# Group B's input projection as seven float32 block products instead of eight, and an earlier copy between the layers

## The reference

```python
for l in range(2):
    h = rms_norm(x, norm1_g[l])
    qa,ka,va, qb,kb,vb, qc,kc,vc = split(h @ w_in[l])        # 2304 columns, 768 for each group A, B, C
    oa = neighbourhood_attention(qa, ka, va)                 # 4 heads of 64
    ob = dilated_attention(qb, kb, vb)                       # 4 heads
    oc = gqa_attention(rope(qc), rope(kc), vc)               # 8 heads, 2 of keys and values
    x = x + [rms_norm(oa) | rms_norm(ob) | rms_norm(oc)] @ w_out[l]
    x = x + hier_moe(rms_norm(x, norm2_g[l]))                # 32 experts, two of one group for each token
```

## Time and profile before

| | us |
|---|---|
| median of 3 runs | 1152.03 (1151.15 to 1152.05) |
| the profiled execution | 1151.47 |
| its span, first to last instruction | 1149.6 |
| TensorE busy in it | 980.4 (85%) |
| VectorE busy | 291.0 (25%) |
| ScalarE busy | 178.7 (16%) |
| DMA, mean rate | 380 GB/s |
| chain that ended last, TensorE's share | 65% |
| the same, DMA's share | 30% |

### The profile page before, as it was taken

The page is one execution under the profiler, slowest core; times in us unless marked ns, Lnnn a source line. Parts: engine busy times, 40 slices in busy tenths (PEclk is TensorE's granted clock), DMA queues, the critical chain, the costliest instruction groups (busy, mean ns, idle before and its releaser), DMA issues.

```text
span 1149.6 us, 13653 instructions
## 1 busy us (share of the span) xinstructions
PE 980.4 (85%) x5402; PEld 460.5 (40%) x5402; DVE 291.0 (25%) x798; ACT 178.7 (16%) x444; POOL 54.0 (5%) x108
## 2 busy tenths in 40 slices
PE   8999999997887947549999999999969779474687
PEld 5556644353343413113356656444524234131242
DVE  4446552111110110001145555421111101100011
ACT  1344311110010100001024343111100001000110
POOL 2121100000000000000021111000000000000000
PEclk9999999999898977868999999999989889787899
DMA  9962999999999999999998248999999999999997
GB/s 319 351 253 110 364 335 421 427 427 428 428 426 427 428 428 427 428 427 421 397 397 312 100 179 351 366 419 427 428 427 428 428 428 427 428 427 428 428 419 290
DMA packets 64760, 437.08 MB, mean 380 GB/s; under 512 B 11230, under 2 KB 15670, under 8 KB 34230
## 3 DMA queue, kind: packets, MB, share of 16 engines
q1 hardware_dynamic: 64645, 436.16, 92.5%
q10 hardware_dynamic: 48, 0.01, 0.0%
HBM read 435.10 MB, written 1.44 MB: 380 GB/s over the span
## 4 chain that ended last, share of the span: by engine, by line
PE 65%; DMA 30%; DVE 2%; SPq 1%; POOL 1%; issue 1%; ACT 0%; POOLq 0%; DVEq 0%
PE bank L1105 33%; DMA ring<-in_w_down 15%; DMA ring<-in_w_gate 10%; PE bank L797 9%; DMA ring<-in_w_up 5%; PE bank L1131 5%; PE bank L929 5%; PE bank L1057 3%; PE bank L756 2%; PE bank L875 1%; PE bank L865 1%; SPq L518 1%; PE bank L897 1%; PE bank L957 1%; PE bank L1123 1%
## 5 line engine op out<-in xcount | busy, mean ns | idle before, releaser
L1105 PE MATMUL bank<-ring,work 128*32 128x512 f32 (+2 forms) x2608 | 481.5, 663 | 135.6 <-DMA ring<-in_w_up 51.2
L1105 PEld LDWEIGHTS bank<-ring,work 128*32 128x32 f32 (+2 forms) x2608 | 145.1, 130 | 400.7 <-issue 398.1
L797 PE MATMUL bank<-ring,hT 128*128 128x512 f32 (+1 forms) x384 | 128.3, 488 | 1.2 <-DVE hT L1474 1.2
L797 PEld LDWEIGHTS bank<-ring,hT 128*128 128x128 f32 x384 | 71.2, 190 | 48.3 <-issue 42.2
L1131 PE MATMUL bank<-work 128*128 128x512 f32 x176 | 81.4, 603 | 2.4 <-ACT work L1427 1.6
L1105 PE MATMUL bank<-work 128*32 128x512 f32 (+1 forms) x176 | 78.2, 594 | 4.1 <-DMA ring<-in_w_up 4.1
L1057 PEld LDWEIGHTS bank<-work,h 128*128 128x128 f32 x640 | 75.1, 192 | 14.5 <-issue 13.7
L1105 PE MATMUL bank<-kept,work 128*32 128x512 f32 (+2 forms) x160 | 68.2, 622 | 13.7 <-DMA ring<-in_w_down 13.7
L1057 PE MATMUL bank<-work,h 128*128 128x128 f32 x640 | 79.1, 277 | 0.0
L1898 DVE COPY work<-bank 128x512 f32<-128x512 f32 x20 | 13.8, 692 | 248.0 <-PE bank L1105 248.0
L1893 DVE TENSOR_TENSOR work<-work,bank 128x512 f32<-128x512 f32 x22 | 15.1, 687 | 213.8 <-PE bank L1105 213.8
(11 more groups left out here) (218 smaller groups left out, 736.0 us busy)
## 6 DMA issues: line engine op xcount, KB each, us to landing
ring<-in_w_gate SPq DMA_DIRECT2D x42, 2048.0 KB, 25.0
ring<-in_w_down SPq DMA_DIRECT2D x38, 2048.0 KB, 23.5
ring<-in_w_up SPq DMA_DIRECT2D x36, 2048.0 KB, 29.7
ring<-in_w_up SPq DMA_DIRECT2D x36, 1024.0 KB, 14.7
ring<-in_w_down SPq DMA_DIRECT2D x28, 1024.0 KB, 10.4
ring<-in_w_gate SPq DMA_DIRECT2D x20, 1024.0 KB, 8.7
ring<-in_w_in SPq DMA_DIRECT2D x8, 1536.0 KB, 12.9
ring<-in_w_out SPq DMA_DIRECT2D x8, 1024.0 KB, 17.1
```

The lines of the kernel that those rows point to most:

```text
L797: last = matmul(bank[6 + i % 2][:, 0:c1 - c0], hT[:, k, t * P:t * P + P], group_in(l, gi)[:, k, c0:c1], start=(k == 0), stop=(k == KD - 1))
L1105: last = nc.tensor.matmul(bank[b][e * w:e * w + w, :], lhs[:, k, e * w:e * w + w], rows(pos, k_count // 2)[:, kk, n * 512:n * 512 + 512], ...
```

## The change

Group B's product is cut in two row blocks, two halves of the features and two halves of the columns: `LEFT` (256 to 640) and `RIGHT` (640 to 768 and 0 to 256, in that order), 384 each. Eight products of blocks, each 4 chunks deep and 384 columns wide, are replaced by seven (`block_1` to `block_7`) of row blocks or their sums with weight blocks or their sums. VectorE forms the four row sums (`rows_summed`), and four weight sums (`term_1` to `term_4`; `term_3` overwrites the right columns of the upper weights). The products are added up in SBUF, scaled by `rstd`, in two buffers `partial(l, t)`: VectorE's steps named `..._added`, `..._kept` and `..._done`, and one on ScalarE (`first_block_kept`). `head_squares` for B reads the finished values in SBUF instead of PSUM. The first output products wait for `v_proj` alone.

Row sums take one piece of the ring and terms with the partial sums three, none of them loaded, until the last columns of B are done (`v_proj`, 12 a layer).

The order on VectorE also changes: `normalised(l, 4)` comes ahead of `greatest(l, 5)`, and the right columns of row block 1 are finished ahead of those of row block 0. Between the layers, `half_turned(1, 0, 1)` moves from ahead of projection 0 to its middle, beside `half_turned(1, 1, 1)`, and the copies of the first two turned parts (`rows_turned`) move from behind the four sums into x to a place between the second and the third.

```diff
@@ -122,7 +122,7 @@
         if key in QUARTERED:
             used[pos] += 3
         for i in range(pos, pos + n):
-            used[i] += i < pos + (2 if n == 3 else 1)
+            used[i] += loaded and i < pos + (2 if n == 3 else 1)
             freed[i], when[i] = done, time
         plan[key] = (pos, [used[i] for i in range(pos, pos + n)], sorted(waits.items()))
...
@@ -133,6 +133,8 @@
             take((l, "in", g), 3, ("p_proj", 12 * l + 4 * g + 4), t0 + 4 * g + 4, ring)
         for n, j in enumerate(OUT_PIECES):
             take((l, "out", j), 1, ("p_out", 12 * l + (4, 4, 8, 12)[n]), t0 + (16, 16, 26, 30)[n], ring)
+        for name, n in (("terms", 3), ("sums", 1)):
+            take((l, name), n, ("v_proj", 12 * l + 12), t0 + 13, ring, loaded=False)
         for n, (name, count, time) in enumerate(BESIDE_FREE):
             freed[PIECES + n], when[PIECES + n] = (name, (l + 1) * count), t0 + time
         for i, it in enumerate(TIME):
...
@@ -337,6 +342,30 @@
         def group_in(l, g):
             pos = PLAN[l, "in", g][0]
             return ring[:, pos * PIECE:(pos + 3) * PIECE].rearrange("p (k c) -> p k c", k=KD)
+        TERM = 4 * 384
+        LEFT, RIGHT = (256, 640), ((640, 768, 0), (0, 256, 128))
+        def row_block(t, half):
+            return hT[:, 4 * half:4 * half + 4, t * P:t * P + P]
+        def row_sum(l, n):
+            pos = PLAN[l, "sums"][0]
+            return ring[:, pos * PIECE + n * 512:pos * PIECE + n * 512 + 512].rearrange("p (k s) -> p k s", k=4)
+        def term(l, n):
+            at = PLAN[l, "terms"][0] * PIECE + n * TERM
+            return ring[:, at:at + TERM].rearrange("p (k c) -> p k c", k=4)
+        def partial(l, t):
+            at = PLAN[l, "terms"][0] * PIECE + 3 * TERM + t * 384
+            return ring[:, at:at + 384]
+        def weight_block(l, half):
+            return group_in(l, 2)[:, 4 * half:4 * half + 4]
         def rows(pos, k):
...
@@ -782,8 +811,7 @@
                     pe.wait_ge(a_sq, 12 * l + i - 1)
                 for k in range(KD):
                     if i == 0 and k == 4:
-                        if l == 0:
-                            half_turned(l, 1, 0)
+                        half_turned(l, *((1, 0) if l == 0 else (0, 1)))
                         half_turned(l, 1, 1)
                     if i < 2 and k % 4 == 0:
                         pe.wait_ge(v_xT, x_turned(l, t, k // 4))
@@ -797,6 +825,57 @@
                     last = matmul(bank[6 + i % 2][:, 0:c1 - c0], hT[:, k, t * P:t * P + P],
                                   group_in(l, gi)[:, k, c0:c1], start=(k == 0), stop=(k == KD - 1))
                 last.then_inc(p_proj, 1)
+            def block_product(b, left, right, done):
+                for lo, src in right:
+                    for k in range(4):
+                        last = matmul(bank[b][:, lo:lo + src.shape[-1]], left[:, k], src[:, k], start=(k == 0), stop=(k == 3))
+                last.then_inc(done, 1)
+            def left_columns(l, half):
+                return ((0, weight_block(l, half)[:, :, LEFT[0]:LEFT[1]]),)
+            def right_columns(l, half):
+                return [(lo, weight_block(l, half)[:, :, c0:c1]) for c0, c1, lo in RIGHT]
+            def block_1(l):
+                pos, count, _ = PLAN[l, "in", 2]
+                pe.wait_ge(landed[pos], 16 * count[0])
+                pe.wait_ge(v_proj, 12 * l + 7)
+                pe.wait_ge(a_sq, 12 * l + 7)
+                block_product(6, row_block(0, 0), left_columns(l, 0), p_block)
+            def block_6(l):
+                pe.wait_ge(v_terms, 4 * l + 2)
+                pe.wait_ge(v_proj, 12 * l + 8)
+                pe.wait_ge(a_sq, 12 * l + 8)
+                block_product(7, row_sum(l, 1), ((0, term(l, 1)),), p_block)
+            def block_2(l):
+                pos, count, _ = PLAN[l, "in", 2]
+                pe.wait_ge(landed[pos + 1], 16 * count[1])
+                pe.wait_ge(v_block, 4 * l + 1)
+                pe.wait_ge(a_block, l + 1)
+                block_product(6, row_block(0, 1), left_columns(l, 1), p_proj)
+            def block_7(l):
+                pe.wait_ge(v_terms, 4 * l + 3)
+                pe.wait_ge(v_block, 4 * l + 2)
+                block_product(7, row_sum(l, 2), right_columns(l, 0), p_block)
+            def block_4(l):
+                pe.wait_ge(v_terms, 4 * l + 4)
+                pe.wait_ge(v_proj, 12 * l + 9)
+                block_product(6, row_block(1, 1), ((0, term(l, 2)),), p_proj)
+            def block_5(l):
+                pe.wait_ge(v_block, 4 * l + 3)
+                block_product(7, row_sum(l, 0), ((0, term(l, 0)),), p_proj)
+            def block_3(l):
+                pe.wait_ge(v_proj, 12 * l + 10)
+                block_product(6, row_sum(l, 3), right_columns(l, 1), p_proj)
             def gains_turned(l, b):
                 if l == 0:
@@ -916,8 +995,7 @@
                 g, t, half = OUTS[n]
                 pos0, chunk0, count = CHUNKS[g]
                 if n < 2:
-                    pe.wait_ge(v_proj, 12 * l + 11 + n)
-                    pe.wait_ge(a_sq, 12 * l + 11 + n)
+                    pe.wait_ge(v_proj, 12 * l + 12)
...
@@ -965,7 +1043,7 @@
                     gains_turned(0, 7)
                 if l == 0:
                     half_turned(l, 0, 0)
-                half_turned(l, 0, 1)
+                    half_turned(l, 0, 1)
                 project(l, 0)
                 project(l, 1)
                 project(l, 2)
@@ -989,19 +1067,22 @@
                 values(l, 1)
                 scores(l, 3)
                 turn_keys(l, 1)
-                project(l, 8)
+                block_1(l)
+                block_6(l)
+                block_2(l)
                 turn_queries(l, 1)
                 softmax_turned(l, 2)
                 softmax_turned(l, 3)
-                project(l, 9)
+                block_7(l)
+                block_4(l)
                 values(l, 2)
                 squares(l, 0)
                 scores(l, 4)
                 values(l, 3)
                 scores(l, 5)
-                project(l, 10)
+                block_5(l)
                 turn_keys(l, 2)
-                project(l, 11)
+                block_3(l)
                 softmax_turned(l, 4)
                 squares(l, 1)
...
@@ -1256,6 +1337,8 @@
             def head_squares(l, i):
                 name, t, (c0, c1) = unit(i)
+                if i >= 10:
+                    t = 11 - i
                 which = ("k" if i % 4 < 2 else "q") + name
                 if which == "qC":
                     dst, n = lengths["qC0" if t == 0 else "qC1"], 512
@@ -1269,7 +1352,19 @@
                     act.wait_ge(p_turn, turned(l, "qA"))
                 if which == "qB":
                     act.wait_ge(v_len, len(LENGTHS) * l + LENGTHS.index("kB") + 1)
+                if name == "B":
+                    activation(dst, qk_b[:, t, c0:c0 + 256], ACT.Square).then_inc(a_sq, 1)
+                    return
                 activation(dst, bank[6 + i % 2][:, 0:n], ACT.Square, scale=rstd[:, t:t + 1]).then_inc(a_sq, 1)
+            def first_block_kept(l):
+                for name, value in PLAN[l, "terms"][2]:
+                    act.wait_ge(frees[name], value)
+                act.wait_ge(g_rstd, rooted(l, "x1"))
+                act.wait_ge(p_block, 3 * l + 1)
+                act.wait_ge(v_block, 4 * l + 1)
+                nc.scalar.mul(partial(l, 1), bank[6][:, 0:384], rstd[:, 1:2]).then_inc(a_block, 1)
             def keys_turned(l, gi):
                 name = "k" + GROUPS[gi]
@@ -1371,6 +1466,7 @@
                 heads_mixed(l, 1)
                 exponentials(l, 3)
                 keys_turned(l, 1)
+                first_block_kept(l)
                 head_squares(l, 8)
                 queries_turned(l, 1)
...
@@ -1468,8 +1564,8 @@
                 nc.vector.tensor_copy(gains[:], bank[b][:, 0:3 * KD]).then_inc(v_gains, 1)
                 dve.wait_ge(v_gains, l + 1)
-            def rows_turned(l):
-                for t, j in ((0, 0), (0, 1), (1, 0), (1, 1)) if l == 0 else BACK:
+            def rows_turned(l, parts):
...
                 b, r = bank[6 + i % 2], rstd[:, t:t + 1]
-                if name == "B":
-                    last = ts(qk_b[:, t, c0:c0 + 256], b[:, 0:256], r, None, ALU.mult)
-                    if c1 > 512:
-                        last = ts(proj[:, t, SEG0["B"] + 512:SEG0["B"] + 768], b[:, 256:512], r, None, ALU.mult)
-                else:
-                    last = ts(proj[:, t, SEG0[name] + c0:SEG0[name] + c1], b[:, 0:c1 - c0], r, None, ALU.mult)
-                last.then_inc(v_proj, 1)
+                ts(proj[:, t, SEG0[name] + c0:SEG0[name] + c1], b[:, 0:c1 - c0], r, None, ALU.mult).then_inc(v_proj, 1)
+            def rows_summed(l):
+                for name, value in PLAN[l, "sums"][2]:
+                    dve.wait_ge(frees[name], value)
+                dve.wait_ge(v_xT, 4 * l + 4)
```

(84 more changed lines are left out.)

5 lines of the change are left out of this document (4 added, 1 removed).

## The result

The changed kernel takes 1155.74 us (median of nine runs, 1154.33 to 1159.50); the kernel before, in nine runs beside it, 1151.58 (1149.90 to 1152.80). The ratio is 1.0037, with an interval of 1.0027 to 1.0048: slower by 0.37%. No run of the one overlaps with a run of the other. The forecast of 1152.7 within 2.3 us is missed, and so are its own bounds of 1151 to 1154.5. The time is inside the wider range of 1149.0 to 1156.3, and within 0.4 us of what the second rival, the falling clock, was priced at.

The account below looks back on a forecast made before the run. VectorE's chain in the mixers, ahead of the continuous DMA stream, was taken as the bound. Waits of +1.3 us and copies of -0.6 made +0.7 on the median 1152.03, about 1152.7 us; range 1149.0 to 1156.3.

Parts of the forecast that it names:

- its own bounds: The forecast time may miss by 0.8 us a layer either way: 1151 to 1154.5 us.
- the second rival, the falling clock: TensorE between 90.5 and 95.2 works little and its clock falls: 1.7 us a layer, 1156.1 us; chance 0.10.
- TensorE's saving: Group B's block products: 18.5 us a layer instead of 20.9, 2.4 spared without waits; kept in full, 1146.6, chance 0.18.
- VectorE's cover: About 13 us more VectorE work a layer stays covered up to block_4; from there VectorE is the bound.
- the chain: VectorE's greatest(5), then ScalarE's copy of turn 4, delay values(4) from 94.53 to 95.2: 0.65 us a layer, +1.3.
- The three rests: TensorE waits of 1.6, 0.6 and 1.3 us between small groups ahead of values(4).
- The copies: Between the layers, the second half of layer 1's projection 0 begins at 581.1 against 581.72: -0.6 us, once.
- The ring: Four pieces held until v_proj 12 release four expert loads later; cost 0, without the DMA gap 2.5 us a piece.
- an uncovered piece: Slow rival: some late loads move by one or two rounds; 4.9 us uncovered gives 1157; chance 0.12, shared with longer chain.
- The price: The falling clock's cost: 64 matmuls after a rest of 4.48 us took 8.73 us against 7.05: 1.7 a layer.
- the slow rivals: Falling clock, 1156.1, chance 0.10; longer chain, 1154.3, or hole in the ring plan, 1157, together chance 0.12.

Follow-up runs that it names:

- the filler's median: Changed kernel with four idle matmul products put into TensorE's three rests ahead of values(4): 1153.26 us, ratio 1.0013.
- the old order: Changed kernel with VectorE's earlier order: greatest(5), right_done(1), normalised(4), right_done(0): 1155.42 us, ratio 1.0029.
- filler in the first rest: Changed kernel with two idle matmul groups ahead of squares(1) alone: 1154.11 us, ratio 1.0020.
- filler in the later rests: Changed kernel with one idle matmul group ahead of turn_queries(2) and one ahead of values(4): 1152.12 us, ratio 1.0000.
- division first with filler, eight products: Kernel before with normalised(4) moved ahead of greatest(5) and four idle products in TensorE's rests: 1155.45 us, ratio 1.0040.
- turn 4 copied first, seven products: Changed kernel with turn 4 copied ahead of exponentials(5) and B's squares, VectorE's half ahead of right_done, values(4) ahead of turn_queries(2): 1148.48 us, ratio 0.9970.
- turn 4 copied first, eight products: Kernel before with turn 4 copied ahead of exponentials(5) and squares, values(4) ahead of turn_queries(2), and the division ahead of greatest(5): 1150.98 us, ratio 0.9993.
- the other pair: Division first plus idle products in the rests, on eight products (1155.45 us) and on seven (1153.26 us): 2.2 us apart by medians, 3.3 each against its own kernel before.

## Why the prediction was right and wrong

**Right, TensorE's saving.** The block products take 0.3225 us an instruction (7.74 us for 24 in the chain), with cut columns 2.79 less the tail of 0.16: 18.2 us a layer, where 18.5 were counted and 20.9 were spent before.

**Right, VectorE's cover.** VectorE's busy time grew by 24.4 us, 12.2 a layer, where 13 were counted, and up to the scores of quad 5 it stayed hidden. The row sums ended 0.33 us before the result that projected(4) waits for, term 2 took 1.82 and projected(7) came at 60.42, and block_7 and block_4 went without a rest (72.81, 75.43). The length of a 1536-element sum was taken as 1.77; it is 1.75. The Trainium skill's formula ("VectorE: DVE Perf Modes", "The TRN2 errata") had given 1.76, and the trace agrees.

**Right, the chain.** With the 0.35 us of start: greatest(5) ended at 90.69 (said: 90.65), turn 4 left TensorE at 90.8 (90.7), the copy was done at 95.0 (95.1), values(4) began at 95.07 (95.2). The three rests were to be 1.6, 0.6 and 1.3 and are 1.56, 0.58 and 0.92. The chain costs 0.54 us in layer 0 and 0.64 in layer 1 (values(4) 1.39 later, projection 0's second half 0.75 later), where 0.65 each were counted. The copies gave 0.70 (0.6). So the traces give 0.54 + 0.64 - 0.70 = +0.5 for the sum without the clock, which was forecast at +0.7; by the filler's median it is +1.4, with an interval of 0.5 to 2.5 that holds both. The ring left no hole: seven transfers were issued from 89.62 on, the last of them at 93.75, and the next two at 115.88, with the DMA share at 0.38 in the window 105 to 115. One sum in the rivals has a slip: 1152.7 and 4.9 us of an uncovered piece are 1157.6, not 1157; nothing hangs on it.

**Wrong, the clock.** The step that failed is the argument that kept the clock out of the sum: "behind a rest of 2.12 us the instruction at 271.00 took 0.59 us, as at 2.4 GHz; my longest is 1.6". The runs showed the clock at its lower level behind rests of 1.56, 0.58 and 0.92 us in both layers, which cost 2.5 us by the medians with and without filler. The argument has two flaws. The rest of 2.12 us was a lone one with dense work on both sides, while the forecast's own rests came three in a row with one-column products and transposes between them: 4.25 us (90.47 to 94.72) in which TensorE works 1.2 and rests 3.06. The forecast wrote that down, "some 1 us in 4.7", and then argued with the longest single rest. And a single row that shows no fall is no bound: behind the old order's rest of 1.98 us, shorter than that of the row, the next group was at half speed in layer 1. How often the clock fell ahead of or at values(4), by the rests from turn 4 on, in the profiled executions:

| kernel | rests, us | layers with the fall |
|---|---|---|
| changed (two executions) | 1.56, 0.58, 0.92 (once 0.46) | 4 of 4 |
| old order, seven products | 1.98, 0.60 or 0.34 | 2 of 2 |
| filler in the first rest | 0.26, 0.58, 0.92 | 1 of 2 |
| filler in the later rests | 1.55, 0.27 or none | 1 of 2 |
| division first, eight products (two executions) | 0.34, 0.34, 1.20 | 1 of 4 |
| before; the same with the ring plan or the copies alone | 0.19, 0.60 | 0 of 6 |
| filler in all, seven products | 0.26, 0.27 | 0 of 2 |
| division first with filler, eight products | none | 0 of 2 |
| turn 4 copied first, seven products | 0.49, 0.94 | 0 of 2 |
| turn 4 copied first, eight products | 0.49, 0.10 | 0 of 2 |

In the three kernels between the first two rows and the last five it falls in some layers and not in others of the same kernel, so there a single profiled execution tells little. The page that the forecast named spoke for the rival: the Trainium skill, "TensorE: Matmul & The Clock Gate", says in "Part 4: PE-mode transpose" that transposes don't count as busy. By it the 0.63 us of the turn drop out too, and the fall is the likelier; the trace agrees with the outcome, but no run took the transposes out alone, so this mechanism is argued, not shown. The Trainium skill's section on the same page, "A second HAM failure mode: psum-queue depth-cycling", tells of another kernel in which many short rests between groups let the clock swing; the trace agrees in so far as the clock fell here with no single rest over 1.56 us. The rival deserved the larger chance.

**The price.** 1.7 a layer was taken from matmuls behind one long rest. Measured from values(4) to the next scores: 1.41 and 2.99 in the two layers of the first execution, 2.44 and 2.96 in those of the second, so 4.4 and 5.4 us an execution; by the medians with and without filler it is 2.5. The two ways do not agree, and no run says why. That the second rival's sum, 1156.1, met the time within 0.4 us is luck in part: in the profiled execution the clock took 4.4 us and not 3.4, the router stage 0.77, which no sum had, while the start was 0.35 earlier and the lateness shrank from 5.24 to 4.3 behind the first expert products of layer 1. It is luck too that the time lies in the range of 1149.0 to 1156.3, which reaches so high only because the slow rivals were priced.

**What the time is made of**, by the runs: the seven products and the copies give 2.5 us (2.2 to 3.3 by the other pair), the division ahead of greatest(5) takes 2.4 by the chain and 4.2 by the median of the old kernel, which holds some falls of the clock, and the clock takes 2.5 on the changed kernel. These do not add up to one sum, as the second and the third overlap. The forecast had netted the first two about rightly, and had not asked what the new order costs alone; that came out only when each was run alone.

**Left open:** whether it is the rests alone or also the transposes between them that let the clock fall; why the falls cost 4.4 and 5.4 us in two traces and 2.5 by the medians; the swing of the idle products in the router stage; whether filler in the later rests alone is really the best; the 1 to 2 us that the division-first order costs beyond its chain.
